# A third PSUM tile for the SSD mixer of a two-block network, with its time sums spread into two banks instead of four

## The chip, the cores and the metric

The kernel runs on one core of one Trainium2 chip. The metric is the device time of one execution in microseconds. A time is the median of several executions of the same program; one further execution was recorded by the hardware profiler, and every row of a profile or trace comes from it. TensorE is called PE here, with PEld for its weight loads, VectorE DVE, ScalarE ACT, GpSimd POOL and SyncE SP.

## The reference, cut to what matters

The program computes two blocks of two layers each, on 512 tokens of width 1024 (16 meta tokens are put in front of them in the first block, so that L = 528). Its first layer is the SSD mixer, the only part that the change touches:

```
z, xbc, dt_raw = split(u @ w_in)                     # z 2048, x 2048, B and C 4 groups of 128, dt 32
xbc = silu(causal_conv4(xbc));  dt = softplus(dt_raw + dt_bias)
a_cs = cumsum(dt * a) in each chunk                  # the sums over time, one row per head (32 heads)
y_diag = (C B^T * exp(a_cs[l] - a_cs[s]) causal) @ (x dt)
state' = state * chunk_decay + B^T (decay_to_end * x dt)
y = y_diag + exp(a_cs) * (C @ state) + x * d_skip
out = rmsnorm_per_group(y * silu(z)) * gate_g @ w_out
h = h + out
```

Behind it come a convolutional FFN, stick-breaking attention, a second FFN, and the second block's two attention layers.

## The kernel before, in words

Everything is held with channels on the 128 partitions and time along the row. A 32-bit matmul of a projection is done as three passes of rounded operands: the weights are split into a high part (`high_part`, L1317, on ACT) and a rest (`piece`, L2365, four pieces on POOL), and lines L694, L695 and L696 are the three passes on PE. A weight unit is 1 MB, loaded by SP into one of two raw slots. Its high part is made on ACT when PE has finished the last tile of the unit two places before it, and its rest on POOL after that; PE waits for the rest (`unit_ready`).

The SSD mixer is one list of 288 steps, `SSD`, written out by `ssd_order()`. Each engine walks the whole list in the same order and does its own part of each step (`pe_step`, `act_step`, `dve_step`, `pool_step`), so that an engine which waits in one step holds back everything behind it in its own queue. 130 of the steps use a PSUM tile of two banks, and `SSD_M` numbers them 0 to 129: the projections B, C, x and z (48 matmul passes each, some 6.1 us), the output projections s (24 passes, some 3.1 us), the transposes bt and xt, gram, l0, the chunk states st, and pair, the output of two heads. Tile M goes into `PS[M % 2]`. `acquire` makes PE wait until tile M-2 has been read, which DVE or ACT tells by `ps_free[M % 2]` (through `signal`, a drain and an increment, L399 to L401, or on the reading instruction itself).

The tiles are read in these lines: B, C and x in L1816 on DVE (followed by the convolution, L1822 and three times L1825), z in L1841, s in L1847 with its addition to the residual in L1849, st in L1907, pair in L1930, xt in L1894 and L1896, gram in L1877. For each head, one matmul (`spread`, L828) copies the head's sums over time to all partitions, in one PSUM bank. Before, these go round four banks, the two of `PC` and the two of `PD`. A spread bank is read twice: by DVE in step decay (L1918, semaphore `dm_full`) and by ACT in step carry (L1411, semaphore `e_full`). ACT's exponentials of step decay are L1404, DVE's product of step weigh L1924, and POOL's product of step carry L2400. PE's matmuls of step pair are L850 (needs little), L854 (behind weigh) and L859 (behind POOL's L2400).

There are four groups of 8 heads. In a group the order is: gram, the norm statistics of the group before (`gate_stats`, L872, then a root on ACT, L1422, and a reciprocal on DVE, L1955), l0, the z tiles and transposes ("z stage"), the first two spreads, then the four states with output projections of the group before and B and C of the next among them ("state stage"), then `through`: per head weigh, the next decay and carry, one or two projection tiles, spread e + 2, and every second head a pair. After head 7 come z of the next group, bt and the last pair ("group end"). The last group is followed by eight s tiles, s(3, 0) to s(3, 7), each with a take-over on DVE (L1685, L1703) that prepares the first FFN, `ffn0`. Its first tile, number 130, has the norm statistics in it (`stats`: three filler matmuls into PD, L674, then the sums, L685).

`PD` also holds the very first product, `dt_sums` (L760), which DVE reads before its semaphore `dtv_full`.

Of the kernel before, what the change touches and what calls it, by code (L numbers as in the profile page):

```python
# [24 lines left out]
L = META + S  # L25
# [114 lines left out]
SSD_M = {}  # L140
# [84 lines left out]
def build(nc, x_in, stream, down, params_in, tables_in, out):  # L225
    ctx = ExitStack()
    with ctx:
# [117 lines left out]
        V0 = BANK - LH  # L345
# [8 lines left out]

        def wide(M):

            return PS[M % 2][:, V0:V0 + L]


        loaded = sem("loaded")  # L360
# [74 lines left out]

        dt_sums = PD[:, :, :].rearrange("p a b -> p (a b)")[:, V0:V0 + L]

# [19 lines left out]
        def spread_of(e):  # L457
            return (PC, PD)[e // 2 % 2][:, e % 2, :]

# [207 lines left out]
        def _(pe):  # L667
# [8 lines left out]
            def stats(name, width, tokens=False):  # L676

                pc = PC[:, :, :].rearrange("p a b -> p (a b)")
                v0 = first_column(width)
                busy({"ffn0": 3, "ffn1": 4, "even": 4, "odd": 4}.get(name, 0), PD[:, 0, :])  # L680
                pe.wait_ge(sem("total_full"), NORM[name] + 1)
                if name == "even":
                    mm(PC[:, 1, 0:S], ones, sq[:, 1, 0:S], start=True, stop=True)
                for a, b in pieces(width):
                    last = mm(pc[:, v0 + a:v0 + b], ones, sd[:, a:b], start=True, stop=True)  # L685
                if tokens:
                    for t, at in enumerate(range(0, width, P)):
                        n = min(P, width - at)
                        last = mm(PD[0:n, 0, t:t + 1], sd[:, at:at + n], ones[:, 0:1], start=True, stop=True)
                last.then_inc(sem("sum_done"), 1)  # L690
# [7 lines left out]
            def project(stage, it, per, j, r, k_n, mcol, moving, high=None, ready=None, within=None):  # L698

                tile = tile_of(stage, j)  # L700
                width = moving.shape[2]
# [40 lines left out]
            def sel(g, e):  # L742

                h = HPG * g + e
                return pick[0:96, h:h + 1].to_broadcast([96, P])

            def pe_step(what, g, j):

                M = SSD_M.get((what, g, j))
                t = PS[M % 2] if M is not None else None  # L750
                if M is not None and what not in ("B", "C", "x", "z", "s"):
                    acquire(pe, "ssd", 0, 2, M)

# [15 lines left out]
                elif what in ("B", "C", "x", "z"):  # L769
                    unit = SSD_UNIT[what, g, j]  # L770
                    unit_ready("ssd", 0, unit)
                    acquire(pe, "ssd", 0, 2, M)
                    mcol = P if what == "C" else P * (j % 2)
# [3 lines left out]
                elif what == "s":  # L777
                    unit = SSD_UNIT[what, g, j]
                    unit_ready("ssd", 0, unit)
                    acquire(pe, "ssd", 0, 2, M)  # L780
                    project("ssd", 0, 1, M, unit, 4, P * (j % 4), x_of(g), y_high(g),
# [39 lines left out]
                elif what == "spread":  # L821
                    n = HPG * g + j
                    if n >= 4:
                        pe.wait_ge(sem("dm_full"), n - 3)
                        pe.wait_ge(sem("e_full"), n - 3)
                    if j == 0 and g:
# [435 lines left out]
        def _(act):  # L1262
# [84 lines left out]
            def act_step(what, g, j):  # L1347

                M = SSD_M.get((what, g, j))
                t = PS[M % 2] if M is not None else None  # L1350
                free = ps_free[M % 2] if M is not None else None

# [319 lines left out]
        def _(dve):  # L1672
            V = nc.vector
            for b in range(2):
                dve.sem_inc(ps_free[b], 1)
            for name, n in (("pd_free", 2),):
# [116 lines left out]
            def dve_step(what, g, j):  # L1793

                M = SSD_M.get((what, g, j))
                t = PS[M % 2] if M is not None else None
                free = ps_free[M % 2] if M is not None else None

# [45 lines left out]
                elif what == "s":  # L1844
# [4 lines left out]
                    V.tensor_tensor(hT[:, j, :], hT[:, j, :], t, ALU.add)  # L1849
                    signal(dve, free, *([h_upd] if g == GROUPS - 1 else []))  # L1850

                elif what == "dtt":
# [769 lines left out]
```

## Time and profile before

| | us |
|---|---|
| median of 3 runs | 2419.88 |
| lowest, highest of the 3 | 2416.62, 2424.52 |
| profiled execution: its span, first to last instruction | 2416.5 |
| PE busy | 2260.2 (94%) |
| DVE busy | 1297.9 (54%) |
| POOL busy | 1008.2 (42%) |
| ACT busy | 923.2 (38%) |

For the profiled execution the page gives the span alone, and no time around it. The span in 40 equal slices of 60.4 us (each digit is the busy share in tenths; PEclk is the granted clock in tenths):

```profile
PE   7888888898999999999998999999998899998897
DVE  7685767788617735235378717733123551016883
PEclk9999999999999999999999999999998999998999
```

The SSD mixer fills the first eight slices and half of the ninth: PE is busy 7 to 8 tenths there and DVE 5 to 8. Rows of a timeline read: start in us, length in us, engine, line, operation, output<-input, shape, count; in brackets the idle time of the engine before the row and what ended it. "DVEq" and "ACTq" are the sequencers of these engines (a drain and an increment). Tile numbers of steps below are those of `SSD_M`.

### The profile page before, as it was taken

The page shows a single profiled execution, that of the slowest core. Times are in us where ns is not written, and L with a number is a line of the kernel's source. Part 1 is how long each engine was busy: PE and PEld are TensorE (multiplying, and loading weights), DVE is VectorE, ACT ScalarE, POOL GpSimd, SP SyncE. Part 2 cuts the span into 40 slices and gives each one's busy share as a digit, 9 for nine tenths or more (in the row PEclk, how much of TensorE's full clock was granted, in tenths as well). Part 3 has the DMA queues.
Part 4 walks back from the last instruction along what each step waited for, and adds up shares of the span by engine and source line. Part 5 has one row for each costly group of instructions (what it writes and reads, how often), then busy time and mean ns, then how long its engine had stood idle before and what let it go on. Part 6 is the DMA issues. An engine that isn't in the chain of part 4 may idle for free.

```text
span 2416.5 us, 38817 instructions
## 1 busy us (share of the span) xinstructions
PE 2260.2 (94%) x15998; PEld 1964.5 (81%) x15998; DVE 1297.9 (54%) x1923; ACT 923.2 (38%) x1481; POOL 1008.2 (42%) x901
## 2 busy tenths in 40 slices
PE   7888888898999999999998999999998899998897
PEld 6788888788999999975698989976885478885565
DVE  7685767788617735235378717733123551016883
ACT  4463636442313333346433313332233431125661
POOL 4443434435545440032245555444345443434641
PEclk9999999999999999999999999999998999998999
DMA  4211111112222222210021232222221011520100
GB/s 157 71 61 63 54 69 58 50 69 71 84 103 87 88 96 88 88 70 1 1 88 71 81 106 90 84 95 87 88 96 62 18 70 70 159 105 36 36 1 35
DMA packets 29374, 175.61 MB, mean 73 GB/s; under 512 B 3984, under 2 KB 4496, under 8 KB 12304
## 3 DMA queue, kind: packets, MB, share of 16 engines
q1 hardware_dynamic: 29200, 173.14, 20.2%
q8 instruction: 127, 2.08, 0.4%
q14 instruction: 47, 0.39, 0.1%
HBM read 166.71 MB, written 2.10 MB: 70 GB/s over the span
## 4 chain that ended last, share of the span: by engine, by line
PE 63%; DVE 13%; issue 8%; POOL 7%; ACT 3%; DVEq 3%; POOLq 2%; SPq 1%; DMA 0%; ACTq 0%
PE PS L694 19%; PE PS L695 18%; PE PS L696 18%; DVE arena L1825 3%; POOL ring_r L2356 2%; PE PS L971 2%; POOL arena L2483 1%; POOL arena L2447 1%; DVE arena L2049 1%; POOLq L2480 1%; DVEq L399 1%; PE PD L1001 1%; ACT arena_r L1317 1%; POOL uT L2459 1%; PE PC L971 1%
## 5 line engine op out<-in xcount | busy, mean ns | idle before, releaser
L696 PE MATMUL PS<-arena_r,ring_r 128*128 128x264 f32 (+3 forms) x3728 | 1138.2, 305 | 0.0
L2356 POOL TENSOR_TENSOR ring_r<-ring,arena_r 128x512 fp32r<-128x512 f32 (+1 forms) x456 | 597.5, 1341 | 864.3 <-ACT arena_r L1317 864.3
L696 PEld LDWEIGHTS PS<-arena_r,ring_r 128*128 128x128 f32 x3728 | 708.2, 190 | 30.7
L694 PE MATMUL PS<-arena_r,arena_r 128*128 128x264 f32 (+3 forms) x2288 | 693.7, 303 | 29.1 <-DVEq L399 10.3
L695 PE MATMUL PS<-arena_r,arena_r 128*128 128x264 f32 (+2 forms) x2256 | 677.5, 300 | 0.0
L694 PE MATMUL PS<-arena_r 128*128 128x264 f32 (+3 forms) x1792 | 556.5, 311 | 19.0 <-ACT arena L1466 4.6
L694 PEld LDWEIGHTS PS<-arena_r,arena_r 128*128 128x128 f32 x2288 | 436.5, 191 | 58.6 <-issue 30.5
L695 PE MATMUL PS<-uT_r,arena_r 128*128 128x264 f32 (+2 forms) x1472 | 461.6, 314 | 0.0
L695 PEld LDWEIGHTS PS<-arena_r,arena_r 128*128 128x128 f32 x2256 | 431.3, 191 | 13.0 <-issue 0.2
L1317 ACT ACTIVATE arena_r<-ring 128x2048 fp32r<-128x2048 f32 (+1 forms) x146 | 262.2, 1796 | 458.8 <-PE PS L696 443.6
L694 PEld LDWEIGHTS PS<-arena_r 128*128 128x128 f32 x1792 | 339.6, 190 | 48.0 <-issue 18.0
L695 PEld LDWEIGHTS PS<-uT_r,arena_r 128*128 128x128 f32 x1472 | 278.4, 189 | 16.8
L2365 POOL TENSOR_TENSOR ring_r<-ring,arena_r 128x512 fp32r<-128x512 f32 x128 | 187.4, 1492 | 216.1 <-ACT arena_r L1317 216.1
L1983 DVE TENSOR_TENSOR hT<-hT,PS 128x512 f32<-128x512 f32 (+2 forms) x56 | 38.8, 693 | 240.1 <-PE PS L696 239.9
L2049 DVE SCALAR_TENSOR_TENSOR arena<-arena,par 128x528 f32<-128x528 f32 (+1 forms) x176 | 155.3, 882 | 13.1
L1729 DVE TENSOR_TENSOR arena<-PS,sd 128x512 f32<-128x512 f32 (+1 forms) x40 | 27.7, 695 | 223.2 <-PE PS L696 223.0
L1440 ACT ACTIVATE arena<-PS 128x528 f32<-128x528 f32 (+1 forms) x76 | 46.0, 606 | 256.8 <-PE PS L696 256.5
L2046 DVE TENSOR_SCALAR arena<-arena,par 128x528 f32<-128x528 f32 (+1 forms) x88 | 78.0, 886 | 69.4 <-ACTq L399 65.0
L695 PE MATMUL PS<-ring_r,arena_r 128*128 128x256 f32 x352 | 99.9, 284 | 0.0
L696 PE MATMUL PS<-arena_r,uT_r 128*128 128x256 f32 x320 | 91.0, 284 | 0.0
L1642 ACT ACTIVATE arena<-arena 128x128 f32<-128x128 f32 (+3 forms) x128 | 71.0, 555 | 39.0 <-DVEq L399 34.5
L1825 DVE SCALAR_TENSOR_TENSOR arena<-arena,par 128x528 f32<-128x528 f32 x72 | 80.1, 1112 | 5.4
(331 smaller groups left out, 2809.6 us busy)
## 6 DMA issues: line engine op xcount, KB each, us to landing
ring<-stream SPq DMA_DIRECT2D x130, 1024.0 KB, 4.8
ring<-down SPq DMA_DIRECT2D x32, 704.0 KB, 4.0
hT<-x_in SPq DMA_DIRECT2D x4, 528.0 KB, 7.2
arena<-tables SPq DMA_DIRECT2D x4, 512.0 KB, 3.8
arena<-arena SPq DMA_DIRECT2D x16, 128.0 KB, 2.4
out<-uT SPq DMA_DIRECT2D x4, 512.0 KB, 2.8
par<-params SPq DMA_DIRECT2D x1, 1634.5 KB, 13.9
arena<-arena SPq DMA_DIRECT2D x8, 136.0 KB, 3.1
```

The lines of the kernel that those rows point to most:

```text
L694: mm(out_, r32(ah), r32(bh), start=start, stop=False)
L695: mm(out_, r32(ah), r32(b), start=False, stop=False)
L696: return mm(out_, r32(a), r32(bh), start=False, stop=stop)
L971: return mm(sb_z(u, e)[:, a:a + rhs.shape[1]], w, rhs, start=False, stop=True, skip_group_check=True)
L1317: A(r32(high_slot(h)[:, 0:width]), raw_slot(h)[:, 0:width], ACT.Copy).then_inc(sem("high_full"), 1)
L1440: A(ffn[raw][:, FCONV - 1:FCONV - 1 + n], tile_of(stage, 2 * r + m)[:, first_column(n):first_column(n) + n], ACT.Copy)
L1642: A(x, x, ACT.Exp, bias=od["nm"][:, n % 4, i:i + 1], scale=-1.0, accum_out=od["rs"][:, n % 4, i:i + 1])
L1825: last = V.scalar_tensor_tensor(cv, raw[:, k:k + L], w(k), cv, ALU.mult, ALU.add)
L2046: V.tensor_scalar(out_, ffn[raw][:, 0:width], w(0), b, ALU.mult, ALU.add)
L2049: last = V.scalar_tensor_tensor(out_, ffn[raw][:, k:k + width], w(k), out_, ALU.mult, ALU.add)
L2356: last = G.tensor_tensor(r32(low[:, cut]), raw[:, cut], split(high[:, cut]), ALU.subtract)
L2365: last = G.tensor_tensor(r32(low[:, cut]), raw[:, cut], split(high[:, cut]), ALU.subtract)
```

## The change

The tiles of the SSD mixer go round three tiles, PS[0], PS[1] and PD. Each has a semaphore of its own, `ssd_free0` to `ssd_free2`; tile M now waits for the reading of tile M-3 (tile 2, the first in PD, for `dtv_full`). The spreads go round the two banks of PC only, so that spread n waits for decay and carry of head n-2 where it waited for those of n-4. ps_free, which the later stages use, is raised in two steps by DVE at the last SSD tiles in PS[0] and PS[1] (129 and 127), and the fillers of `ffn0` wait until PD's last SSD tile (128) has been read.

```diff
-        def wide(M):
-            return PS[M % 2][:, V0:V0 + L]
+        PD_flat = PD[:, :, :].rearrange("p a b -> p (a b)")
+        def ssd_tile(M):
+            return (PS[0], PS[1], PD_flat)[M % 3]
+        def ssd_free(M):
+            return sem(f"ssd_free{M % 3}")
+        def ssd_freed(n):
+            return len([M for M in range(len(SSD_M)) if M % 3 == n])
...
         def spread_of(e):
-            return (PC, PD)[e // 2 % 2][:, e % 2, :]
+            return PC[:, e % 2, :]
...
                 v0 = first_column(width)
+                if name == "ffn0":
+                    pe.wait_ge(sem("ssd_free2"), ssd_freed(2))
                 busy({"ffn0": 3, "ffn1": 4, "even": 4, "odd": 4}.get(name, 0), PD[:, 0, :])
...
-                tile = tile_of(stage, j)
+                tile = ssd_tile(j) if stage == "ssd" else tile_of(stage, j)
...
+            def ssd_acquire(M):
+                if M == 2:
+                    pe.wait_ge(sem("dtv_full"), 1)
+                if M >= 3:
+                    pe.wait_ge(ssd_free(M), M // 3)
...
-                    acquire(pe, "ssd", 0, 2, M)
+                    ssd_acquire(M)
...
                     n = HPG * g + j
-                    if n >= 4:
-                        pe.wait_ge(sem("dm_full"), n - 3)
-                        pe.wait_ge(sem("e_full"), n - 3)
+                    if n >= 2:
+                        pe.wait_ge(sem("dm_full"), n - 1)
+                        pe.wait_ge(sem("e_full"), n - 1)
...
-                t = PS[M % 2] if M is not None else None
-                free = ps_free[M % 2] if M is not None else None
+                t = ssd_tile(M) if M is not None else None
+                free = ssd_free(M) if M is not None else None
...
-            for b in range(2):
-                dve.sem_inc(ps_free[b], 1)
...
                     signal(dve, free, *([h_upd] if g == GROUPS - 1 else []))
+                    if M + 3 >= len(SSD_M) and M % 3 < 2:
+                        dve.sem_inc(ps_free[M % 3], 1 + (len(SSD_M) + 1 - M % 3) // 2)
```

## Rows read from the trace of the kernel before

**Rows 1.** Busy time of stretches: us, each engine's busy time (count), granted clock, DMA share, GB/s.
```profile
25.00:510.00 485.00, 428.40 (x3502) 397.12 (x3501) 357.77 (x450) 236.58 (x350) 206.77 (x144) 0.98 0.17 62
210.30:213.70 3.40, 3.40 (x18) 3.40 (x17) 0.86 (x2) 0.00 (x0) 0.00 (x0) 0.50 0.00 0
281.90:285.30 3.40, 3.40 (x34) 3.07 (x32) 0.00 (x0) 0.43 (x1) 0.00 (x0) 0.51 0.79 282
```
**Rows 2.** Who waited for whom, PE, 25 to 510 us: total, times, longest.
```profile
PE PS L694 <- DVEq L399: 14.4, 12, 2.3
PE PS L850 <- DVEq L401: 9.8, 3, 4.2
PE PS L843 <- DVE arena L1907: 3.8, 3, 1.3
...
PE PS L694 <- POOL ring_r L2365: 3.3, 3, 1.3
...
PE PS L802 <- DVEq L401: 0.2, 1, 0.2
```
**Rows 3.** The same for DVE, 25 to 510 us.
```profile
DVE arena L1816 <- PE PS L696: 33.4, 11, 5.1
DVE arena L1841 <- PE PS L696: 29.6, 9, 4.3
DVE PS L1847 <- PE PS L696: 17.3, 12, 3.3
```
**Rows 4.** Timeline of PE: the first matmul of tiles 7, 10 and 29.
```profile
61.72 0.36 PE L694 MATMUL PS<-arena_r 128*128 128x264 f32 x1 [1.83 <-DVEq L399]
71.33 0.21 PE L809 MATMUL PS<-arena 128*16 128x16 f32 x2 [1.89 <-ACTq L401]
140.43 0.29 PE L850 MATMUL PS<-arena 16*64 16x16 f32 x4 [2.42 <-DVE arena L1930]
```
**Rows 5.** Timeline of PE at a group end: tile 65.
```profile
281.52 0.29 PE L850 MATMUL PS<-arena 16*64 16x16 f32 x4 [4.24 <-DVEq L401]
```
**Rows 6.** Timeline of DVE at the group ends of tiles 65 and 97.
```profile
280.28 0.71 DVE L1841 TENSOR_TENSOR arena<-PS,sd 128x528 f32<-128x528 f32 x1
285.31 0.76 DVE L1930 SCALAR_TENSOR_TENSOR arena<-arena,par,PS 128x528 f32<-128x528 f32 x1 [4.32 <-PE PS L859]
...
404.86 0.77 DVE L1930 SCALAR_TENSOR_TENSOR arena<-arena,par,PS 128x528 f32<-128x528 f32 x1 [2.41 <-PE PS L859]
```
**Rows 7.** Timeline of PE: tiles 49, 50, 52 and 54.
```profile
208.09 1.13 PE L843 MATMUL PS<-arena 128*128 128x512 f32 x2 [1.32 <-DVE arena L1907]
209.84 0.36 PE L694 MATMUL PS<-arena_r,arena_r 128*128 128x264 f32 x1 [0.63 <-DVEq L399]
221.60 0.39 PE L694 MATMUL PS<-arena_r,arena_r 128*128 128x264 f32 x1 [1.25 <-POOL ring_r L2365]
230.19 0.36 PE L694 MATMUL PS<-arena_r,arena_r 128*128 128x264 f32 x1 [2.25 <-DVEq L399]
```
**Rows 8.** Timeline of ACT (carry of head 0 of group 2) and PE (spread of head 2).
```profile
349.06 0.60 ACT L1411 ACTIVATE arena<-PC 128x512 f32<-128x512 f32 x1
348.49 0.40 PE L828 MATMUL PD<-acs_parts,pick 96*128 96x512 f32 x1
```
**Rows 9.** Timeline, group 3: PE (spread of head 6), ACT (carry of head 4).
```profile
458.17 0.40 PE L828 MATMUL PD<-acs_parts,pick 96*128 96x512 f32 x1
460.35 0.57 ACT L1411 ACTIVATE arena<-PC 128x512 f32<-128x512 f32 x1
```
**Rows 10.** Timeline of DVE: three instructions of a convolution, twice.
```profile
326.65 2.46 DVE L1825 SCALAR_TENSOR_TENSOR arena<-arena,par 128x528 f32<-128x528 f32 x3
375.00 5.41 DVE L1825 SCALAR_TENSOR_TENSOR arena<-arena,par 128x528 f32<-128x528 f32 x3
```
**Rows 11.** Timeline at the hand-over: DVE (tile 129 read), PE (fillers, sums of `ffn0`).
```profile
510.93 0.70 DVE L1849 TENSOR_TENSOR hT<-hT,PS 128x528 f32<-128x528 f32 x1
514.49 2.74 PE L674 MATMUL PD<-par 128*128 128x512 f32 x6
518.84 1.16 PE L685 MATMUL PC<-sd,par 128*128 128x264 f32 x4 [1.61 <-DVEq L399]
```

More of the change, by code:

```diff
@@ L434, in build @@
         sums = PC[:, :, :].rearrange("p a b -> p (a b)")[:, V0:V0 + L]
-        dt_sums = PD[:, :, :].rearrange("p a b -> p (a b)")[:, V0:V0 + L]
+        dt_sums = PD_flat[:, V0:V0 + L]
         def x_of(g):
@@ L771, in pe_step @@
                     unit_ready("ssd", 0, unit)
-                    acquire(pe, "ssd", 0, 2, M)
+                    ssd_acquire(M)
                     mcol = P if what == "C" else P * (j % 2)
@@ L779, in pe_step @@
                     unit_ready("ssd", 0, unit)
-                    acquire(pe, "ssd", 0, 2, M)
+                    ssd_acquire(M)
                     project("ssd", 0, 1, M, unit, 4, P * (j % 4), x_of(g), y_high(g),
@@ L1349, in act_step @@
                 M = SSD_M.get((what, g, j))
-                t = PS[M % 2] if M is not None else None
-                free = ps_free[M % 2] if M is not None else None
+                t = ssd_tile(M) if M is not None else None
+                free = ssd_free(M) if M is not None else None
                 if what in ("B", "C", "x", "z", "s") and last_of_unit((what, g, j)):
@@ L1795, in dve_step @@
                 M = SSD_M.get((what, g, j))
-                t = PS[M % 2] if M is not None else None
-                free = ps_free[M % 2] if M is not None else None
+                t = ssd_tile(M) if M is not None else None
+                free = ssd_free(M) if M is not None else None
                 if what == "dt":
```

## The prediction

> **What bounds the kernel now.** I read the busy time by stretches first, then the waits of PE and of DVE, then the timelines. The change touches only the SSD mixer, from 25 to 510 us. In these 485 us PE is busy for 428.4 and DVE for 357.8, at a mean granted clock of 0.98 [rows 1]: PE is the fuller engine, but neither is full. The waits say why. PE waits 14.4 us in 12 places for a projection tile to be released by DVE, 9.8 us in 3 places for the tile of a pair, 3.8 us for the tile of a state; the thirteen rows of this answer that are releases of a tile, down to the last of 0.2 us, add to 41.8 us [rows 2]. DVE in turn waits 33.4, 29.6 and 17.3 us for projections that PE has not finished [rows 3]. Each of the two waits for the other at different times, with only two tiles between them. What a third tile can give at most is those 41.8 us and the slow clock that follows the longer waits; what it can't give is time in which DVE is the busy one and PE needs DVE's data.
>
> **The third tile, place by place.** I follow both engines through the list of steps with the lengths that they have now, and note how much earlier the step at the end of each stretch comes.
>
> Head, to 109 us. Tiles 2 and 3 no longer wait, but tile 4 waits for the POOL split of its weights, which is not earlier, so that nothing of this stays. From there tile 7 waited 1.83 us and tile 10 1.89 us [rows 4]; with the smaller ones up to tile 23, which are among those of rows 2, it is 7.7 us. DVE's chain behind the time sums (dtt, end, the three parts) moves only by what tile 7 gives, 1.3 us, and tile 11 then by 2.3. DVE's states then hold PE back less than the tiles did. I keep 5.4.
>
> To 163 us. Tile 29 waited 2.42 us [rows 4] and tile 33 2.80. DVE is the busy engine here, so PE's earlier pairs only shorten the group end, where DVE reads the pair at once instead of waiting. The sum is 7.8 against 5.4: I keep 2.4.
>
> Group ends of groups 1 and 2. DVE reads z at 280.28; only then is tile 63 released, and PE starts the pair, tile 65, after 4.24 us idle [rows 5]; DVE waits for that pair for 4.32 us [rows 6]. With three tiles the pair has its tile since tile 62 was read and its data too (all weigh and carry steps are over), so that it is done under the wait for z. DVE goes straight on: 4.3 us less here, less 0.5 for gram, which now is what waits for z's tile: 3.8. At the other end the wait is 2.41 us [rows 6], of which I keep 2.2. Together 6.0.
>
> State stages. Tile 49 waits 1.32 and tile 50 0.63 us [rows 7], because two short tiles stand behind a convolution of 4 us on DVE. With three tiles the state goes ahead of it. After these waits tile 50 runs at half clock: in 210.3 to 213.7 the granted clock is 0.50 [rows 1], 1.2 GHz, and its 24 passes take 4.7 us instead of 3.1. Group 1: 0.9 + 1.1 from waits and 1.6 from the clock, 3.6. Group 2 has the same waits at full clock: 2.0. Group 3 has three longer ones (0.8, 1.5, 0.9): 1.8 kept. Together 7.4.
>
> Tiles 52 to 55 and 84 to 87. The wait of 1.25 us of tile 52 is POOL's weight split [rows 7], counted from the tile that freed the raw weights, and stays. Tile 54 waits 2.25 us [rows 7]; it goes, but here the spread takes part of it back (next part). With the clock, which drops in group 1 alone, I keep 2.2 and 0.8, together 3.0.
>
> The z stages (0.4, 0.6 and 0.3 us in each of three groups): the DVE reciprocal and the spread hold most of it, 0.3 kept each, together 0.9.
>
> Sum of the gains: 5.4 + 2.4 + 6.0 + 7.4 + 3.0 + 0.9 = 25.1 us.
>
> **The spreads in two banks.** Removed or added work: none, 32 matmuls of 0.40 us each stay. What is added is that the spread of head n waits for the ACT exponential of head n-2. In groups 1 and 2 that binds for the third spread: it now starts at 348.49, while ACT reads carry of head 0 from 349.06 to 349.66 [rows 8], so that PE would wait 1.2 us, 0.95 after the shift of its surroundings. Tile 86 stands behind it in PE's queue. It is in the 2.2 and 0.8 above. From the fourth spread on there is a tile of 3.1 or 6.1 us between, and carry is done. Where no tile stands between two spreads (head 6 of groups 0 and 3), PE reaches the spread at 458.17 and ACT finishes carry of head 4 at 460.92 [rows 9]. The wait of 2.3 us is in PE's queue before a pair that had to wait for POOL's product until 460.9 anyway; the pair ends 1.5 us later, and DVE reads it only at 463.66. The cover is thus DVE's own lateness; without it the whole 1.5 would count. I take 0.2 for group 3 and nothing for group 0, where the later group end covers it. Both ends of the cost for 24 spreads (heads 2 to 7): nothing, or 2.3 us each, 55 us, if every one were like rows 9.
>
> **The hand-over to ffn0.** Tile 130 uses PS[0]. Before, that was released by tile 128; now tile 129 is in PS[0], which DVE has read at 511.63 [rows 11]. So its first 42 passes, 5.1 us, run from 511.7 instead of 508.5 and end at 516.9; three fillers of 2.74 us [rows 11] end at 519.6, and the sums start there instead of at 518.84: 0.8 us late. PE has idled 4 us before, and behind such an idle time the clock is at 0.51 now [rows 1, 5]: half of 3.4 us is 1.7 more. Between 0.8 and 2.5 I take 1.5. From there on PE is full, so it isn't hidden. The wait of the fillers for PD costs nothing, since tile 128 is read before tile 129; tile 2's wait for `dtv_full` ends before DVE reads tile 0, for which it waits now. The two added increments of DVE are 0.1 us at most.
>
> The clock once more: PE's idle time is not gone but cut in smaller parts, and a slow stretch may come up elsewhere. One of 3.4 us costs 1.7; I put 1.6 in for it. So 25.1 - 0.2 - 1.5 - 1.6 = 21.8 us, span 2416.5 - 21.8 = 2394.7. The profiled execution has no time of its own beside its span, and the median of the runs stands 3.4 us above it: 2398 us.
>
> DVE and POOL get in each other's way. Three L1825 take 2.46 us with POOL quiet and 5.41 us beside its four pieces [rows 10], 1 us more each. The Trainium skill, "SBUF — State Buffer" (Who interferes with whom), says that VectorE and GpSimd share a port pair under an exclusive lock, held for the whole instruction; the trace agrees, with these two rows. When PE runs ahead, POOL's pieces fall on other DVE instructions, but their number is the same, so I take zero from this, with 10 us either way (ten instructions of 1 us) as bounds.
>
> **Rivals.**
> DVE is the bound. If what PE gains is only handed on where DVE itself stood idle for a pair, there remain the three group ends (2.4 + 3.8 + 2.2) and 2 to 3 us of the head, less the hand-over: some 10 us, 2410. For it: beside POOL a convolution takes DVE 5.41 us [rows 10] with the reading and a weigh and decay still to come, against 6.1 us for the tile on PE, so in `through` it has hardly a pause. Against: it waits 80 us for projections [rows 3].
>
> Nothing is gained. PE's 41.8 us of waits [rows 2] turn into waits for data: for the weights' split (3.3 us now, rows 2, which does not get faster), for carry, for weigh. Then the time is 2418, the hand-over alone against one group end. The Trainium skill, "TensorE: Matmul & The Clock Gate" (HAM oscillation), reports a kernel that gained no more from double-buffered PSUM (126.6 to 125.5 us) once its loads were in order; by it this case would be this one. No row here shows a third tile; against it speak the 4.3 us of DVE's own wait in rows 6, which two tiles alone explain.
>
> Slower. The spreads' wait, above: ACT comes to carry late because it makes 1.9 us weight splits, loads tables of 1.28 us and does Silu between the exponentials, and it is in order; PE waits for it in the middle of its list, and all projections, and so DVE's work, stand behind. It decides from 1 us per spread on average (24 us for 24). At 1.9 us each, near to the 2.3 of rows 9, it is 45 - 23 = 22 us more than before: 2442.
>
> **How the numbers follow.** The forecast 0.62, DVE as the bound 0.20, nothing gained 0.12, slower 0.06. The forecast's own range is 2390 to 2407, from the bounds of DVE against POOL (10 us), cut a little since they add up partly. The range given is 2389 to 2412: it takes in the first rival and leaves out the two others. A change of this kernel can be told from none at about 0.3%, 7.3 us, that is below 2412.6 or above 2427.1. Faster 0.82 (the forecast and nearly all of the first rival), same 0.12, slower 0.06.
>
> **What would show it.** The waits of PE for DVE's releases (41.8 us) should fall below 12 in the mixer. DVE's wait for the pair at the group ends (4.32, 2.41) should be under 0.3, and gram, not the pair, should be what waits. Tile 54's 2.25 us should be gone, with a wait of about 1 us for ACT L1411 before L828 in its place. Tile 52 and 84 should keep 1.1 to 1.3 us for POOL. The granted clock of the mixer should rise from 0.98 to 0.99. The sums of `ffn0` should come 22 us earlier, and their distance from the last s tile should grow by 1 to 2 us. After the mixer nothing should change. The forecast is wrong if L828 waits for ACT by more than 10 us in all, if DVE's own busy time grows by over 10 us, or if the clock falls in more stretches than before.

## The result, and the profile after

The changed kernel takes 2394.64 us, the median of 4 executions (2392.01 to 2396.31), beside 2418.25 us for the kernel before on the same chip (2410.03 to 2424.52). The ratio is 0.9879, with a 95% interval of 0.9857 to 0.9900: 24 to 35 us of 2419.88. Run a second time on another chip it had 0.9887 (0.9871 to 0.9902). The forecast of 2398 us is 3.4 us above the median and inside its own range, but as a saving its 21.8 us (a ratio of 0.991) lie short of both intervals.

The busy time of stretches in the changed kernel (us, each engine's busy time and count, granted clock, DMA share, GB/s). The first line answers to [rows 1], the others are the stretches of the mixer in which the clock was low:

```profile
25.00:510.00 485.00, 446.58 (x3654) 419.03 (x3653) 374.80 (x470) 245.60 (x357) 218.39 (x151) 0.97 0.18 64
47.00:50.50 3.50, 3.16 (x14) 3.16 (x15) 3.10 (x5) 0.30 (x1) 0.29 (x1) 0.51 0.55 171
357.70:364.50 6.80, 6.02 (x43) 5.69 (x44) 6.36 (x9) 5.27 (x9) 1.44 (x2) 0.50 0.43 157
381.50:385.00 3.50, 3.50 (x18) 3.50 (x18) 2.58 (x6) 2.30 (x4) 0.00 (x0) 0.51 0.18 75
432.70:439.60 6.90, 6.59 (x46) 5.82 (x47) 4.90 (x6) 1.92 (x6) 2.67 (x3) 0.51 0.38 146
456.60:460.10 3.50, 3.41 (x14) 2.67 (x13) 2.76 (x2) 0.70 (x1) 0.41 (x1) 0.51 0.56 176
483.90:490.80 6.90, 5.39 (x24) 5.42 (x25) 6.39 (x6) 3.75 (x4) 5.62 (x4) 0.51 0.01 2
```

From 25 us up to the sums of `ffn0` PE does the same matmuls (3539 on record in each trace) in 470.6 us where it took 494.0, with 38.4 us of idle time in place of 58.7. In this profile the clock did not rise: six stretches at half clock add to 31 us, where before there were six with 24 us. In the second profiled execution of the changed kernel they are 24 us as well.

Who waited for whom, PE, 25 to 510 us (total, times, longest), the changed kernel, against [rows 2]:

```profile
PE PC L846 <- ACT arena L1429: 9.1, 7, 2.8
PE PS L705 <- POOL ring_r L2383: 5.9, 3, 3.3
PE PS L705 <- issue: 5.3, 1, 5.3
PE PS L872 <- DVE arena L1942: 4.0, 2, 2.7
PE PS L827 <- DVEq L410: 3.9, 2, 2.2
...
PE PD L827 <- DVEq L410: 1.6, 1, 1.6
```

The large waits for a projection's tile and for a pair's tile (14.4 and 9.8 us) are gone. Most of what remains are waits for data: the spread (L846, before L828) for ACT's carry, the rest of the weights from POOL, weigh for the pair. Releases are left at gram (L827, 5.5 us), ahead of six projections that follow short tiles (L705 behind DVE L1914 and L1925 and an ACT reading, 4.6 us in rows not shown, none over 1.1 us), and in the 5.3 us ahead of tile 130. The same view for DVE, against [rows 3]:

```profile
DVE arena L1832 <- PE PS L707: 20.8, 7, 4.3
DVE arena L1857 <- PE PS L707: 15.2, 5, 4.8
DVE arena L1832 <- PE PD L707: 10.9, 4, 4.3
DVE arena L1857 <- PE PD L707: 8.6, 4, 3.3
DVE PS L1863 <- PE PS L707: 4.7, 3, 1.9
```

A group end, against [rows 5, 6], in the timelines of PE and of DVE of the changed kernel (start, length, engine, line, ...):

```profile
261.29 0.29 PE L868 MATMUL PD<-arena 16*64 16x16 f32 x4
265.64 0.21 PE L827 MATMUL PS<-arena 128*16 128x16 f32 x2 [2.17 <-DVEq L410]
...
264.76 0.71 DVE L1857 TENSOR_TENSOR arena<-PS,sd 128x528 f32<-128x528 f32 x1
265.68 0.77 DVE L1948 SCALAR_TENSOR_TENSOR arena<-arena,par,PD 128x528 f32<-128x528 f32 x1 [0.21 <-issue]
```

The pair starts without a wait, is done under DVE's other work, and DVE reads it 0.21 us after z instead of 4.32. It is gram now that waits.

To see where the time came from, I took the end of each numbered tile in both traces and the difference to the kernel before. Its change over a stage is what that stage gave (minus) or cost:

```
stage (tiles)                       forecast   changed kernel   second run of it
head (0-23)                            -5.4        -5.0             -5.1
to 163 us (24-36)                      -2.4        -2.3             -2.3
z stages (37-41, 69-73, 101-105)       -0.9        -4.0             -3.9
state stages (42-50, 74-81, 106-116)   -7.4        -9.9             -9.9
tiles 51-55, 82-87                     -3.0        -3.5             -3.5
group end of group 1 (63-68)           -3.8        -4.3             -4.3
group end of group 2 (93-100)          -2.2        +1.0             -3.7
spread and pairs, group 3 (117-122)    +0.2        +2.8             +2.6
s tiles (123-129)                       0          -3.1             -2.4
hand-over (130)                        +1.5        +5.0             +3.8
a slow stretch somewhere               +1.6         (within the stages)
sum                                   -21.8       -23.4            -29.0
```

Tiles 56 to 62 and 88 to 92 gave 0.2 us and are left out; after tile 130 the difference of the first run stays the same to 0.01 us (tile 134), so that there nothing happens behind the mixer. The span fell from 2416.5 to 2393.4 us. In the second run it is 2382.9 us, 33.6 less: 4.6 us of that lie behind tile 130, where the change does nothing.

### The profile page after: what moved, and what is told of

Same layout as the page of the kernel before. It is cut to its first block, busy times and chain, and to the rows that moved or that the text cites. A ratio compares the mean times of both kernels' runs of the same rounds, so it can differ in the third digit from the quotient of the medians.

```text
span 2393.4 us, 38818 instructions
## 1 busy us (share of the span) xinstructions
PE 2255.6 (94%) x15998; PEld 1965.5 (82%) x15998; DVE 1295.5 (54%) x1923; ACT 923.6 (39%) x1481; POOL 1009.7 (42%) x901
## 4 chain that ended last, share of the span: by engine, by line
PE 66%; DVE 10%; issue 8%; POOL 7%; ACT 3%; DVEq 2%; POOLq 2%; SPq 1%; DMA 0%; ACTq 0%
PE PS L705 18%; PE PS L706 18%; PE PS L707 18%; POOL ring_r L2374 2%; DVE arena L1841 2%; PE PS L989 2%; POOL arena L2501 1%; POOL arena L2465 1%; DVE arena L2067 1%; PE PD L705 1%; POOLq L2498 1%; PE PD L706 1%; PE PD L707 1%; PE PD L1019 1%; POOL uT L2477 1%
## 5 line engine op out<-in xcount | busy, mean ns | idle before, releaser
L707 PE MATMUL PS<-arena_r,ring_r 128*128 128x264 f32 (+2 forms) x3408 | 1047.5, 307 | 0.0
L705 PE MATMUL PS<-arena_r,arena_r 128*128 128x264 f32 (+3 forms) x2192 | 663.3, 303 | 19.8 <-DVE arena_r L2034 5.2
L707 PEld LDWEIGHTS PS<-arena_r,ring_r 128*128 128x128 f32 x3408 | 648.3, 190 | 30.6
L706 PE MATMUL PS<-arena_r,arena_r 128*128 128x264 f32 (+2 forms) x2160 | 648.2, 300 | 0.0
L705 PE MATMUL PS<-arena_r 128*128 128x264 f32 (+3 forms) x1568 | 495.2, 316 | 17.0 <-issue 5.3
L705 PEld LDWEIGHTS PS<-arena_r,arena_r 128*128 128x128 f32 x2192 | 416.2, 190 | 43.2 <-issue 16.4
L706 PEld LDWEIGHTS PS<-arena_r,arena_r 128*128 128x128 f32 x2160 | 410.6, 190 | 13.4 <-issue 0.7
L706 PE MATMUL PS<-uT_r,arena_r 128*128 128x264 f32 (+2 forms) x1248 | 400.4, 321 | 0.0
L705 PEld LDWEIGHTS PS<-arena_r 128*128 128x128 f32 x1568 | 300.4, 192 | 39.6 <-issue 9.2
L706 PEld LDWEIGHTS PS<-uT_r,arena_r 128*128 128x128 f32 x1248 | 239.2, 192 | 17.3 <-issue 0.5
L707 PE MATMUL PD<-arena_r,ring_r 128*128 128x264 f32 x320 | 91.1, 285 | 0.0
```

The lines of the kernel that those rows point to most:

```text
L705: mm(out_, r32(ah), r32(bh), start=start, stop=False)
L706: mm(out_, r32(ah), r32(b), start=False, stop=False)
L707: return mm(out_, r32(a), r32(bh), start=False, stop=stop)
```

## The experiments

Each is the changed kernel with an edit, unless said otherwise; ratios are to the kernel before, on the same chip. The two tiles of before with the spreads in two banks:

```diff
+SSD_SLOT = [m % 2 for m in range(len(SSD_M))]
-            return (PS[0], PS[1], PD_flat)[M % 3]
+            return (PS[0], PS[1], PD_flat)[SSD_SLOT[M]]
```

> Two tiles as before, but the spreads in two banks as after: the cost of the spread half of the change by itself. Theory (the spread's wait for carry of head n-2 costs where no tile or little PE work stands between two spreads, and DVE's and PE's lateness covers most): 0 to 3 us slower than before, 2418 to 2422, with PE's L846 waiting for ACT L1429 by 3 to 8 us in all; with two tiles PE comes to the spreads later, so less than the 9.1 us of the kernel after. Rival (the wait holds PE and everything behind it, so that the third tile has paid for it): 8 us or more slower, ratio above 1.003.

Measured: 2420.76 us, ratio 0.9993 (0.9974 to 1.0011). The spreads alone change nothing that can be told. In the trace the wait is longest at the spread of head 6 of group 3:

```profile
467.18 0.77 PE L849 MATMUL PC<-acs_parts,pick 96*128 96x512 f32 x1 [2.72 <-ACT arena L1432]
```

With it the waits of this kind are 7.4 us in 5 places. The pair behind this one runs at half clock, and by ends of tiles the stage costs 2.7 us, as much as in the changed kernel (2.8). Over 12 executions that doesn't show beside the noise. So the third tile carries the gain.

The third tile at three group ends only:

```diff
+for _m in (33, 65, 97):
+    SSD_SLOT[_m] = 2
```

> The third tile only for the last pair of groups 0, 1 and 2 (tiles 33, 65, 97), two tiles for all else, spreads in two banks. Theory (each place has its own gain, and these three give what DVE waited for the pair): 2.3 + 3.8 + 2.2 = some 8 us faster than before less what the spreads cost: 2408 to 2413. Rival, DVE is the bound everywhere and the group ends are all that the change gives: as fast as the kernel after, 23 to 29 us faster than before. Rival, only tiles in rotation help: no difference from before.

Measured: 2423.70 us, ratio 1.0000 (0.9981 to 1.0019), no gain. Pair 65 does come 5.9 us earlier than tile 62 lets expect, and two tiles later all of it is gone: gram waits for its tile 3.1 us, and behind that wait the clock is low.

```profile
284.29 0.24 PE L832 MATMUL PS<-arena 128*16 128x16 f32 x2 [3.10 <-ACTq L414]
```

The stretch behind it (us, busy times, granted clock, ...):

```profile
283.50:293.80 10.30, 9.51 (x45) 9.47 (x46) 4.23 (x9) 3.49 (x6) 0.00 (x0) 0.50 0.30 104
```

That is 10.3 us at a granted clock of 0.50, 1.2 GHz. With the third tile for gram, l0 and z behind the pair too, as in the changed kernel, the gain stays. How much of the loss here is gram's wait and how much the clock's, this run doesn't separate.

The third tile in the state stages and the s tiles behind them (tiles 42 to 55, 74 to 87, 106 to 114), two tiles elsewhere:

```diff
+for _a, _b in ((42, 56), (74, 88), (106, 115)):
+    for _m in range(_a, _b):
+        SSD_SLOT[_m] = (0, 1, 2)[(_m - _a) % 3]
```

> The third tile only from the first state of groups 1, 2 and 3 on to the tile before the first pair (tiles 42 to 55, 74 to 87, 106 to 114), two tiles elsewhere, spreads in two banks. Theory: the state stages and the s tiles behind them give the larger part, 4.3 + 2.7 (group 1), 2.8 + 1.1 (group 2) and 3 (group 3), by the trace of the kernel after: 10 to 14 us faster than before, 2404 to 2408. Rival (the gain of a state stage is only PE running ahead, and is given back in the stage behind, where DVE is the busy engine): under 4 us faster.

Measured: 2411.62 us, ratio 0.9950 (0.9932 to 0.9968), 12 us. By ends of tiles these stages gave 4.2 + 2.6 + 3.0 + 0.9 + 2.7 = 13.4 us, the same as in the changed kernel to 0.05 us each. They are independent of the rest.

The third tile up to tile 41, two behind it:

```diff
+SSD_SLOT = [m % 3 if m < 42 else m % 2 for m in range(len(SSD_M))]
```

> Three PSUM tiles up to tile 41 only, two behind that, the spreads in their two banks throughout. Theory: the sum's terms are at their places, and what a stage gains stays gained until a stage behind it waits for something else: in the profile of the changed kernel the start of the mixer up to tile 41 stands 8.6 us earlier than before (6.3 were forecast for it: the head, the stretch up to 163 us and no end of group 0). So 2411 to 2415 us, a ratio of 0.995 to 0.998. Rival: with two tiles behind it the gain is given back, as the group ends' was when they had the third tile alone; then the ratio is 0.998 to 1.001, and the gains are no sum of places.

Measured: 2411.05 us, ratio 0.9946 (0.9926 to 0.9967). The gain of the head stays until tile 92 (8.5 us early there), so the rival falls; behind it the spread of group 3 and a low clock leave 4.3 us at tile 130 in the profiled execution. By the ratios, 0.0050 and 0.0054 below 1, this run and the one before it make 25 of the 24 to 35 us; by ends of tiles the two parts are 8.5 and 13.4 us, 22 together. The intervals, some 4 us either way each, don't tell these sums apart.

The hand-over with the last tile in PD, which tile 130 doesn't need:

```diff
+SSD_SLOT = [m % 3 for m in range(len(SSD_M))]
+SSD_SLOT[125:] = [0, 2, 0, 1, 2]
```

> The kernel after, with the last five tiles of the mixer placed so that tile 129 is in PD, 128 in PS[1] and 127 in PS[0]: ffn0's first tile no longer waits for the reading of tile 129. Theory (the hand-over gives back 3.3 us, by 5.3 us of waiting and half the clock behind it): 3 to 4 us faster than the kernel after, ratio to before 0.9865, and the sums of ffn0 within 0.3 us of DVE's last addition. Rival (DVE's total is what the sums wait for anyway): no difference from the kernel after.

Measured: 2385.96 us, ratio 0.9862 (0.9832 to 0.9892). The interval overlaps the changed kernel's; the trace is clearer. Tile 130 in the changed kernel, and in this one (PE, first passes):

```profile
484.39 0.70 DVE L1865 TENSOR_TENSOR hT<-hT,PS 128x528 f32<-128x528 f32 x1
485.41 0.56 PE L705 MATMUL PS<-arena_r 128*128 128x264 f32 x1 [5.29 <-issue]
```

```profile
488.77 0.39 PE L708 MATMUL PS<-arena_r 128*128 128x264 f32 x1 [2.30 <-DVE uT_r L1705]
```

In the changed kernel PE stands for 5.29 us until DVE has read tile 129 out of PS[0], and then works at half clock until 490.8. With the other slots it starts tile 130 at once, waits 2.30 us within it for the data, and by the ends of tiles the hand-over costs 1.6 us (1.9 to 3.0 in three later kernels with this edit), where it costs 3.8 to 5.8 in the four that have the change's own slots.

The changed kernel again:

> The changed kernel as it is, timed beside the three variants of it on one chip. Every theory expects the ratio of before, near 0.988 (2391 to 2397 us). It fixes two things that single profiles leave open: whether the wait ahead of tile 117 (3 us ending with the spread of head 6 of group 3) and the 4 to 5 us that are given back between tile 129 and tile 130 are there in a second execution, and which of the half-clock stretches come again (those at tile 4 and behind tile 129 should, if idle time ahead of a fixed wait makes them; those at 357.7 and 381.5 us need not).

Measured: 2395.75 us, ratio 0.9887 (0.9871 to 0.9902). The longest waits repeat to 0.2 us:

```profile
PE PC L846 <- ACT arena L1429: 7.9, 6, 2.8
PE PS L705 <- POOL ring_r L2383: 5.8, 3, 3.3
PE PS L705 <- issue: 5.1, 1, 5.1
```

The half-clock stretches at tile 4, ahead of tile 117 and at tile 130 come again (46.8, 429.1, 480.3 us); that at 381.5 does not, and two others come instead (128.8 and 449.6 us). So group 2's end has its gain here (3.7 us). The 4.7 us that lie between it and the loss in the table are mostly the clock's: the first profile has 6.8 us more at half clock there, and weigh came 1.2 us later.

The spread behind the pair where no tile stands between:

```diff
-            out += [("spread", g, e + 2)] if e + 2 < HPG else []
+            behind = e and e % 2 == 0 and not tiles.get(e)
+            out += [("spread", g, e + 2)] if e + 2 < HPG and not behind else []
             if e and e % 2 == 0:
                 out += [("pair", g, e // 2 - 1)]
+                out += [("spread", g, e + 2)] if e + 2 < HPG and behind else []
```

> The changed kernel with one order changed: where no tile stands between two pairs of heads (head 4 of groups 0 and 3, head 2 of group 0), the next spread is issued behind the pair's matmul and not ahead of it. Theory: with two banks the spread of head 6 of group 3 waits for ACT's read of head 4's bank, PE stands 2.8 us ahead of tile 117 and 3.8 us are given back there; behind the pair the spread finds its bank free, tile 117 is 2 to 4 us earlier, and the kernel is 1 to 4 us faster than the changed kernel (ratio to before 0.9865 to 0.9875 where that has 0.988). Rival: the pair itself waits for GpSimd's product and for DVE, PE's wait only changes its name, and the time is the changed kernel's within 1 us. Second rival: the spread comes too late for ACT's use of it, and the next tile waits as long as before.

Measured: 2391.08 us, ratio 0.9865 (0.9850 to 0.9881), not to be told from the changed kernel. Both happen, theory and second rival, each in its group. In group 3 the time from the end of tile 116 to the pair's first matmul falls from 3.7 to 0.2 us. In group 0 the next spread comes too late and waits for ACT itself, and tile 29 starts 2.8 us later than in the changed kernel:

```profile
139.33 0.76 PE L848 MATMUL PC<-acs_parts,pick 96*128 96x512 f32 x1 [3.27 <-ACT arena L1431]
140.02 0.40 PE L870 MATMUL PD<-arena 16*64 16x16 f32 x4
```

This order and the other slots together:

> The order of the run before this one, together with the other slots of the last five tiles (the last tile in the third PSUM tile, whose reader doesn't hold up the next stage). Theory: the two costs are at different places and add up; the hand-over gave some 3.5 us, the spread 1 to 4, so 2387 to 2391 us, a ratio to before of 0.984 to 0.986. Rival: what is saved at tile 117 is lost again ahead of tile 130, since DVE's chain of reads sets the time of the hand-over; then it has the time of the run with the other slots alone.

Measured: 2393.82 us, ratio 0.9874 (0.9854 to 0.9894). Missed: no better than either alone. Its five executions have the lowest mean clock of the kernels with three tiles throughout (0.973), with 44 us at half clock in the profiled mixer. The waits had changed and the clock had taken it back, so the clock itself was tried next. To this last kernel 13 short matmuls were added (the program's own fillers, two passes of 0.59 us each) where PE idles longest: 3 at tile 4, 2 at the gram of each of three groups, 4 at the last norm statistics. The expectations count the two at gram once and so speak of nine.

```diff
+                    if M == 4:
+                        ssd_acquire(M)
+                        pe.wait_ge(sem("loaded_b"), 16)
+                        busy(3, t[:, 0:BANK])
                     unit_ready("ssd", 0, unit)
...
+                if what == "gram" and g:
+                    pe.wait_ge(sem("dm_full"), HPG * g)
+                    pe.wait_ge(sem("e_full"), HPG * g)
+                    busy(2, PC[:, 0, :])
...
+                if g == GROUPS - 1:
+                    busy(4, PC[:, 0, :])
                 pe.wait_ge(sem("ga_full"), g + 1)
```

> The kernel of the run before this one with nine short matmuls more that compute nothing that is used: 3 ahead of tile 4's wait for GpSimd, 2 ahead of the gram of groups 1 to 3, 4 ahead of the last wait of the gate's sums. Theory: what the changed kernel fell short of is that half-clock stretches follow PE's waits (31 us of half clock in the mixer, 24 before, where fewer were forecast); with PE busy in those places the stretches at tile 4 and at the groups' ends are gone, the mean granted clock rises by 0.002 to 0.003, and the time falls by 3 to 6 us against the run before this one. Rival: the stretches come wherever PE idles for a few us anywhere, these places aren't special, the mean clock doesn't move and the fillers cost up to 2 us. Second rival: the total of half-clock time is a matter of the chip's load and not of PE's waits; then the stretches wander to other tiles and the time is unchanged.

Measured: 2382.20 us, ratio 0.9820 (0.9802 to 0.9837), 11.6 us below the run before it, where 3 to 6 were expected. Half-clock time in the profiled mixer is 14 us instead of 44.

The fillers alone, in the changed kernel:

> The changed kernel with the nine fillers and nothing else. Theory: the clock of the mixer is lost where PE idles 2 to 4 us ahead of a wait; the mean clock over the runs is 0.978 to 0.980 (the changed kernel 0.975), worth 1.8 us per 0.001, less 1 to 2 us for the fillers: 2387 to 2391 us, a ratio of 0.985 to 0.987. Rival: the clock gained in the kernel with all the edits came with the other two edits, not with the fillers; then it has 0.988 and a clock of 0.975.

Measured: 2386.88 us, ratio 0.9848 (0.9826 to 0.9871), mean clock of its runs 0.9792, where the changed kernel has 0.9753 and 0.9752. The theory holds, at the upper end of what it expected. Tile 4 in the timeline of PE, of the changed kernel and then of this one:

```profile
47.34 0.59 PE L705 MATMUL PS<-arena_r 128*128 128x264 f32 x1 [3.32 <-POOL ring_r L2383]
47.73 0.42 PE L706 MATMUL PS<-uT_r,arena_r 128*128 128x264 f32 x1
```

```profile
43.83 2.74 PE L683 MATMUL PS<-par 128*128 128x512 f32 x6
47.30 0.39 PE L705 MATMUL PS<-arena_r 128*128 128x264 f32 x1 [0.74 <-POOL ring_r L2393]
47.53 0.29 PE L706 MATMUL PS<-uT_r,arena_r 128*128 128x264 f32 x1
```

The stretches there and around the gram of group 3 in this one:

```profile
47.00:50.50 3.50, 3.20 (x26) 3.20 (x27) 3.14 (x5) 0.34 (x1) 0.25 (x1) 1.00 0.56 178
376.80:386.80 10.00, 10.00 (x73) 8.70 (x72) 5.41 (x10) 4.14 (x7) 1.02 (x1) 1.00 0.29 105
```

Tile 4 starts at the same time, and its passes take 0.29 us instead of 0.42: 26 of them fit into 3.5 us where 14 did. Of the nine profiled executions with three tiles in the head, the six without fillers have a half-clock stretch here and the three with them have none.

All three edits, the order changed in group 3 alone:

```diff
+            behind = g == GROUPS - 1 and e == 4
```

> The changed kernel with all three edits: the spread of head 6 behind the pair in group 3 alone, the other slots for the last five tiles, the nine fillers. In the run with the order changed in groups 0 and 3, the third pair of group 0 came 4.2 us late (its spread came too late) while tile 117 of group 3 came 3.7 us early. Theory: without the edit in group 0 the 4 us are there, so it is 2 to 5 us faster than the run with the nine fillers before it (2377 to 2380 us, a ratio of 0.979 to 0.981). Rival: the 4 us of group 0 are hidden by its last pair's wait for DVE, and the time is that run's within 1 us.

Measured: 2381.39 us, ratio 0.9829 (0.9806 to 0.9851). By the times it is the run with the fillers before it within 1 us, as the rival had it. In its trace tile 130 is 4.2 us earlier than there, and the granted clock of the mixer is 1.00, the first slow stretches coming behind it (517.9 and 534.9 us); five executions don't settle which of the two views is right.

```profile
25.00:510.00 485.00, 458.43 (x3777) 423.73 (x3776) 383.65 (x484) 250.15 (x362) 222.32 (x153) 1.00 0.19 66
```

Both are faster than the changed kernel, by 13 us in the medians.

The kernel before with the same fillers:

> The kernel before with the same nine fillers. It tells whether the fillers pay only where the change made PE wait longer in one place. Theory: before, PE idled in many short waits of 0.3 to 1 us and the half-clock stretches of the mixer (24 us) fall at other tiles than the fillers' places (none of the six is at tile 4; three are behind the groups' ends), so the fillers bring 0 to 3 us: a ratio of 0.998 to 1.000. Rival: the fillers are worth the same here as in the changed kernel (5 us or more, a ratio of 0.996 to 0.998): then clock lost ahead of the gram is no matter of the change.

Measured: 2421.58 us, ratio 0.9998 (0.9977 to 1.0019), the median of 12 executions (one of them took 5553 us, which the median doesn't feel). No gain, as the theory had it, but not for its reason. The mean clock of the eleven others rose to 0.976, from 0.973. With two tiles tile 4's slot is free late, so that the fillers push the tile back: it starts at 49.39 us instead of 47.30.

```profile
47.12 2.84 PE L674 MATMUL PS<-par 128*128 128x512 f32 x6 [0.47 <-DVEq L399]
```

So the clock is also to be had in the kernel before, but there the fillers stand in the way at tile 4; whether that is all that eats up the gain was not tried.

## Why the prediction came out so

*What bounds it.* Right. PE's waits for releases of tiles, 41.8 us, are 10.1 now in the mixer (5.5 for gram, 4.6 for projections) and under the 12 foretold, with 5.3 more for tile 130, which the forecast had as the hand-over. Waits for data took their place in part, 9.1 us of them the spreads', so that PE's idle time fell by 20 us. Of the signs of being wrong none came: L828's waits stay under 10 us, DVE's busy time is the same (1297.9 and 1295.5 us), and the low stretches are six as before. "DVE is the bound" and "nothing is gained" fall by their own numbers: 24 us and more, in stages between the group ends. The Trainium skill, "TensorE: Matmul & The Clock Gate" (HAM oscillation), reports a kernel for which double buffering in PSUM gave no further gain; this case does not follow it, with 1.2% from a third tile.

*Head and to 163 us.* Right to 0.4 us. Tile 4 waits for POOL, as said, but the three short waits of tiles 2 to 4 are now one of 3.32 us, with 3.4 us of half clock behind it (1.4 us).

*Group ends.* Right: 4.3 against 3.8, and 3.7 against 2.2 in the second run (a loss of 1.0 in the first). The pair waits no more, gram does.

*State stages and tiles 51 to 87.* The mechanism is right, the size low (9.9 against 7.4). By groups it is 4.3, 3.0 and 2.7 us against 3.6, 2.0 and 1.8: too little was kept in each, and in group 3 I had halved the three waits. Tiles 52 and 84 keep the wait for POOL, and tile 54's has turned into one of the spread for ACT, as foretold (the changed kernel):

```profile
208.70 0.39 PE L705 MATMUL PS<-arena_r,arena_r 128*128 128x264 f32 x1 [1.27 <-POOL ring_r L2383]
...
215.94 0.47 PE L846 MATMUL PC<-acs_parts,pick 96*128 96x512 f32 x1 [1.14 <-ACT arena L1429]
```

*The z stages.* Wrong in size, and the largest single miss on the side of the gains: "the DVE reciprocal and the spread hold most of it". They hold none. All of 0.4 + 0.6 + 0.3 us came out in each group, 1.3 us three times, to 0.05 us.

*The spreads.* The step that failed is the price of 0.2 us that rests on "The cover is thus DVE's own lateness". The wait was seen (2.3 us, measured 2.80), and the cover is there: counted from the end of tile 116, DVE came to this pair after 5.6 us in the kernel before, and comes after 6.0 now. What was left out is the clock behind the wait, which the forecast did count at the hand-over. The kernel with the third tile at three group ends has the same wait and full clock behind it. Its pair is done 1.6 us later than before (1.5 were forecast), DVE reads it without a wait, and the stage costs 0.5 us:

```profile
465.43 0.47 PE L851 MATMUL PC<-acs_parts,pick 96*128 96x512 f32 x1 [2.73 <-ACT arena L1434]
466.04 1.09 PE L877 MATMUL PS<-sq,arena 128*64 128x128 f32 x16
468.32 0.75 DVE L1953 SCALAR_TENSOR_TENSOR arena<-arena,par,PS 128x528 f32<-128x528 f32 x1
```

In the changed kernel the pair's matmuls run at half clock, the pair is done 3.8 us later than before, and DVE waits for it:

```profile
432.29 0.57 ACT L1429 ACTIVATE arena<-PC 128x512 f32<-128x512 f32 x1
433.01 0.76 PE L846 MATMUL PC<-acs_parts,pick 96*128 96x512 f32 x1 [2.80 <-ACT arena L1429]
434.03 1.98 PE L872 MATMUL PS<-sq,arena 128*64 128x128 f32 x16
437.76 0.76 DVE L1948 SCALAR_TENSOR_TENSOR arena<-arena,par,PS 128x528 f32<-128x528 f32 x1 [1.79 <-PE PS L877]
```

So the stage costs 2.6 to 2.8 us instead of 0.2. With two tiles all through (the first experiment) it costs the same 2.7, so that this price is the spreads' and doesn't come from a DVE that the third tile made earlier. With the spread behind the pair it costs 0.2 us, and with the fillers as well it gives 0.5. The rival of a slower kernel had this wait in PE's path, and was wrong in how often it is paid: 9.1 us in 7 places, not 24 spreads.

*The hand-over and the s tiles.* These belong together: DVE's take-overs set the time of tile 130, so what PE gains on the s tiles (3.1 and 2.4 us in the two runs, none was forecast) it loses again there. The net cost is 2.0 and 1.3 us, against the 1.5 of the sum. The fillers of the changed kernel come 21.5 us and its sums 23.3 us earlier than before [rows 11]:

```profile
493.02 2.74 PE L683 MATMUL PD<-par 128*128 128x512 f32 x6
495.59 1.05 PE L696 MATMUL PC<-sd,par 128*128 128x264 f32 x4
```

The sign that was foretold, 1 to 2 us more between the last s tile and the sums, was badly chosen: it is 5.1 us (15.5 against 10.3), 3.1 of them the s tiles' own.

*The clock.* "The granted clock of the mixer should rise from 0.98 to 0.99" did not come in the profiles: it is 0.97 and, in the second, 0.98, with 31 and 24 us at half clock where 24 were before, though PE's idle time is down by 20 us. Single profiles can't settle it. Over all executions with a clock on record the mean of the whole program is 0.975 in 9 of the changed kernel and 0.973 in 55 of the kernel before; by the line fitted at the end, an estimate, some 4 us of the saving are this rise. So the 1.6 us that were put in as a loss were not needed. "PE's idle time is not gone but cut in smaller parts" was wrong: waits that were spread over several tiles had become single ones of 3 to 5 us, at tile 4, ahead of tile 117 and at tile 130, and there the stretches come in both runs. The kernels with fillers bear out that such waits cost clock: 15 executions with a mean clock of 0.980 against 9 of the changed kernel with 0.975.

The sum against the second run: z 3.0, states 2.5, the tiles and the two group ends 2.5 us more than forecast, and the 1.6 us for the clock not needed, less 2.4 for the spread; that makes the 7.2 us between 21.8 and 29.0. The terms that were sized too low are thus first the z stages (0.9 put, 4.0 measured) and the state stages (7.4 and 9.9). In the first profiled run the end of group 2, mostly by its low clock, took 4.7 us of it back, so that its 23.4 us look nearer to the forecast than the two ratios, by which the saving is about a quarter larger than forecast. That the 2398 us come within 3.4 us of the median is luck in part: misses of both signs cancel in it.

## What to carry to other kernels

One more buffer gives most of what the waits for releases show, stage by stage, and also the small ones count in full where nothing else is late; at one point of the list alone (the group ends) it gave nothing, since the next tile then waited. When a cost is put at nothing because another engine is late anyway, ask how long the cover lasts if the clock is low behind the wait: here it held at full clock (0.5 us) and not at half (2.8 us). Look where the waits that remain add up to single ones of 3 us and more, above all at the last tile of a stage, and fill or reorder these: here that was worth 13 us, beside the 24 to 35 of the change.

## What the runs showed of the hardware

The time of one program goes with the mean granted clock: in 29 executions of the kernel before on one chip, from 2412 to 2432 us, a fitted line falls by 1.8 us for each 0.001 of it.

At tile 4 a wait of 3.32 us is followed by 3.4 us at 1.2 GHz, in both runs of the changed kernel; where PE spent 2.74 us of it on matmuls that nobody needs, the clock stayed at 2.4 GHz. A shorter wait can have a stretch beside it too. The one at 357.7 us (357.5 in the second run, and there in two of the three kernels with fillers) begins within PE's wait for weigh, from 355.74 to 358.48 us:

```profile
358.48 1.97 PE L872 MATMUL PS<-arena 128*64 128x128 f32 x16 [2.74 <-DVE arena L1942]
```

In the second run this wait is 1.54 us. In the kernel with the fillers alone a stretch at 82.1 us has only a wait of 0.77 us just ahead of it. But not every wait has one: the 2.73 us ahead of tile 117 in the kernel with the third tile at the group ends are followed by full clock, and so are the 2.68 us at tile 130 in the kernel with all three edits.

What sets a stretch off and what spares one is open. The Trainium skill, "TensorE: Matmul & The Clock Gate" (A second HAM failure mode: psum-queue depth-cycling), describes short idle times between groups of matmuls that go round PSUM banks, and a clock that falls with them; no run here tells whether it is this.
